# A four-layer encoder trunk: the two halves of a seven-product down-projection, product by product

## The reference

```python
for i in range(DEPTH):
    h = _rmsnorm(x, norm_mix[i])
    y = ...                      # mixer i % 3
    x = x + y
    x = x + _squared_relu_mlp(_rmsnorm(x, norm_mlp[i]), mlp_w1[i], mlp_w2[i])
return _rmsnorm(x, norm_final)

def _squared_relu_mlp(h, w1, w2):          # w1: 1024 x 4096, w2: 4096 x 1024
    return jnp.square(jax.nn.relu(h @ w1)) @ w2
```

## Time and profile before

| | |
|---|---|
| median of three runs | 2018.82 us (2018.57 to 2020.11) |
| the profiled execution's own time | 2018.45 us |
| its span, first to last instruction | 2016.7 us |
| PE busy | 1975.1 us (98%) |
| DVE busy | 1572.5 us (78%) |
| ACT busy | 1100.7 us (55%) |
| POOL busy | 346.7 us (17%) |
| read from HBM | 248.21 MB |

### The profile page before, as it was taken

One profiled execution on the slowest core, in us unless ns is written; L12 is line 12 of the kernel. 1 busy time (PEld: TensorE's weight loads), 2 busy tenths in 40 slices (PEclk: granted clock), 3 DMA queues, 4 the chain that ended last, 5 costly groups with the idle time before them and its releaser, 6 DMA issues.

```text
span 2016.7 us, 31611 instructions
## 1 busy us (share of the span) xinstructions
PE 1975.1 (98%) x12912; PEld 1779.3 (88%) x12912; DVE 1572.5 (78%) x1898; ACT 1100.7 (55%) x1540; POOL 346.7 (17%) x403
## 2 busy tenths in 40 slices
PE   9999999999999999999999999999999999999998
PEld 7888899999878889999888889999988888899997
DVE  7866878885898878887598786888687758688874
ACT  6655534545466645455456663554647646354463
POOL 7002001110200201113731201111731011011100
PEclk9999999999999999999999999999999999999999
DMA  6122457765222266667332145685632123468761
GB/s 192 63 67 72 140 136 167 194 141 162 89 85 91 87 157 157 159 155 184 119 88 71 58 151 139 165 205 141 169 86 71 57 69 126 110 166 189 173 189 42
DMA packets 232352, 256.31 MB, mean 127 GB/s; under 512 B 19632, under 2 KB 191216, under 8 KB 232208
## 3 DMA queue, kind: packets, MB, share of 16 engines
q1 hardware_dynamic: 183024, 207.01, 32.2%
q0 software_dynamic: 46784, 45.89, 14.6%
q10 hardware_dynamic: 2400, 1.38, 0.2%
HBM read 248.21 MB, written 2.10 MB: 124 GB/s over the span
## 4 chain that ended last, share of the span: by engine, by line
PE 84%; DVE 11%; ACT 3%; issue 2%; DMA 0%; SPq 0%; DVEq 0%; ACTq 0%
PE psum L772 26%; PE psum L774 25%; PE psum L773 25%; DVE w_lo L1611 2%; PE psum L1245 2%; DVE u_lo L1844 1%; ACT w_hi L2663 1%; DVE arena_r L1844 1%; DVE x L1901 1%; PE psum L1218 1%; DVE arena L1850 1%; PE psum L1353 1%; DVE h_lo L1638 1%; PE psum L1194 1%; PE psum L1190 1%
## 5 line engine op out<-in xcount | busy, mean ns | idle before, releaser
L1611 DVE TENSOR_TENSOR w_lo<-w_raw,w_hi 128x1024 fp32r<-128x1024 f32 x339 | 415.1, 1232 | 193.7 <-ACT w_hi L2663 192.3
L2663 ACT ACTIVATE w_hi<-w_raw 128x1024 fp32r<-128x1024 f32 x343 | 358.4, 1058 | 367.3 <-PE psum L774 237.4
L772 PE MATMUL psum<-u_hi,w_hi 128*128 128x512 f32 (+1 forms) x1256 | 439.9, 350 | 12.0 <-DVE u_lo L1844 7.4
L772 PE MATMUL psum<-h_hi,w_hi 128*128 128x256 f32 (+1 forms) x1368 | 440.6, 322 | 1.1 <-DVE w_lo L1611 1.1
L773 PE MATMUL psum<-h_lo,w_hi 128*128 128x256 f32 (+1 forms) x1368 | 437.3, 320 | 0.0
L774 PE MATMUL psum<-h_hi,w_lo 128*128 128x256 f32 (+1 forms) x1368 | 437.3, 320 | 0.0
L774 PE MATMUL psum<-u_hi,w_lo 128*128 128x512 f32 (+1 forms) x1256 | 433.9, 345 | 0.0
L773 PE MATMUL psum<-u_lo,w_hi 128*128 128x512 f32 (+1 forms) x1128 | 398.4, 353 | 0.0
L773 PE MATMUL psum<-arena_r,w_hi 128*128 128x256 f32 x1184 | 331.8, 280 | 0.0
L772 PEld LDWEIGHTS psum<-h_hi,w_hi 128*128 128x128 f32 x1368 | 260.1, 190 | 21.1 <-DVE w_lo L1611 1.6
L773 PEld LDWEIGHTS psum<-h_lo,w_hi 128*128 128x128 f32 x1368 | 260.4, 190 | 19.1 <-issue 1.2
(11 more groups left out here) (380 smaller groups left out, 3208.0 us busy)
## 6 DMA issues: line engine op xcount, KB each, us to landing
w_raw<-in_mlp_w SPq DMA_DIRECT2D x204, 512.0 KB, 4.9
arena<-in_mlp_w SPq DMA_DIRECT2D x92, 512.0 KB, 4.9
w_raw<-in_mlp_w POOLq DMA_DIRECT2D x52, 512.0 KB, 6.1
arena<-in_mlp_w POOLq DMA_DIRECT2D x28, 512.0 KB, 6.0
w_raw<-in_mla_w_o SPq DMA_DIRECT2D x16, 512.0 KB, 3.5
w_raw<-in_lru_w_in SPq DMA_DIRECT2D x16, 512.0 KB, 4.0
w_raw<-in_swa_w_in SPq DMA_DIRECT2D x12, 512.0 KB, 3.9
w_raw<-in_mla_w_ukv SPq DMA_DIRECT2D x8, 512.0 KB, 4.2
```

What stands on the lines that cost most here:

```text
L772: nc.tensor.matmul(out, stat[0], mov[0], start=start, stop=False, skip_group_check=skip)
L1611: ins = nc.vector.tensor_tensor(w_lo[:, to], tile, exact(w_hi[:, to]), ALU.subtract)
L2663: nc.scalar.activation(w_hi[:, to], raw_tile(op.raw), ACT.Copy).then_inc(w_hi_done, 1)
```

## The change

`seven_down(0)` and `seven_down(1)` become one `both_down`. PE now runs the first product of half 0, the first of half 1, the second of half 0, and so on; each left operand serves two products in a row. All four areas are claimed within the first four products. `weight_plan` lists operands and transfers in the new order. DVE's queue is written anew: a split for each product, the additions to `x` by halves, and the four areas freed after the last four products, in the order 1, 3, 0, 2. Its operand UT4 is made after U22 instead of before. Neither the number of matmuls nor that of the other instructions changes.

```diff
-    def seven_down(i, s, g):
+    def both_down(i, s):
...
-        a, e, b, p, q = blocks_of(block)
-        raws.extend((a, q, b, p, e))
...
+        halves = blocks(0), blocks(1)
+        for order in (0, 4, 2, 3, 1):
+            raws.extend(half[order] for half in halves)
+        for a, e, b, p, q in halves:
+            ops.append(Operand("A11", a))
+            a.freed = len(ops)
+        for a, e, b, p, q in halves:
+            ops.append(Operand("A21+A22", q))
+            q.freed = len(ops)
+        for a, e, b, p, q in halves:
+            ops.append(Operand("A12", b))
+        for a, e, b, p, q in halves:
+            ops.append(Operand("A11+A21", p, (p, e)))
+        for g, (a, e, b, p, q) in enumerate(halves):
+            ops.append(Operand("A11+A21+A22", p, made=sums + 1 + g))
+            down_sums.append((b, p))
+        for a, e, b, p, q in halves:
+            ops.append(Operand("A22", e))
+            p.freed = e.freed = len(ops)
+        for g, (a, e, b, p, q) in enumerate(halves):
+            ops.append(Operand("A11+A12+A21+A22", b, made=sums + 3 + g))
+            b.freed = len(ops)
+        sums += 4
...
+X_FIRST, X_V, X_Y, X_Z, X_SECOND = (1, 2), (3, 5), (7, 8), (9, 10), (11, 13)
...
+            def both_down():
...
+                halves = (0, 1), (2, 3)
+                for g, (xy, own) in enumerate(halves):
+                    claim(xy)
+                    pe.wait_ge(u_turned, n + 1)
+                    group(bank(xy, 0), U11, False)
+                for g, (xy, own) in enumerate(halves):
+                    claim(own)
+                    pe.wait_ge(u_turned, n + 2)
+                    group(bank(own, 1), UT1, False)
...
+                for g, (xy, own) in enumerate(halves):
+                    pe.wait_ge(u_turned, n + 7)
+                    pe.wait_ge(x_added, 7 * d + X_SECOND[g] + 1)
+                    group(bank(xy, 0), U22, True)
...
+            def both_down(n):
...
+                u_low(n, 3, U21)
+                dve.wait_ge(u_squared, 4 * n + 4)
+                nc.vector.tensor_tensor(kept[0][1], kept[0][1], kept[1][1], ALU.subtract).then_inc(u_turns, 1)
+                dve.wait_ge(u_high, 7 * n + 2)
+                nc.vector.tensor_tensor(minus_t1, minus_t1, kept[1][1], ALU.subtract).then_inc(u_turns, 1)
+                split(1)
                 product_passed()
...
+                add_first(0)
+                u_low(n, 4, UT3)
+                dve.wait_ge(u_turns, 4 * n + 3)
+                nc.vector.tensor_tensor(kept[1][0], kept[1][0], minus_t1, ALU.add).then_inc(u_turns, 1)
                 product_passed()
...
+                add_first(1)
+                split(1)
+                u_low(n, 5, UT2)
                 product_passed()
+                split(1)
+                add_v(0)
+                u_low(n, 6, U22)
                 product_passed()
...
+                split(1)
+                add_v(1)
+                u_low(n, 7, UT4)
+                product_passed()
+                split(1)
+                add_y(0)
+                product_passed()
+                split(1)
+                add_y(1)
+                product_passed()
                 add_blocks(*down_sums[d])
...
+                split(1)
+                add_z(0)
                 product_passed()
+                add_blocks(*down_sums[d + 1])
+                split(1)
+                add_z(1)
                 product_passed()
+                add_second(0)
+                split(1)
                 product_passed()
+                add_second(1)
+                split(1)
+                product_passed()
+                free(add(x21[0], Z[0], X_SECOND[0] + 1), 1)
+                split(1)
+                product_passed()
+                free(add(x21[1], Z[1], X_SECOND[1] + 1), 3)
+                split(1)
+                product_passed()
+                free(add(x12[0], X[0], X_V[0] + 1), 0)
+                split(1)
+                product_passed()
+                free(add(x12[1], X[1], X_V[1] + 1), 2)
+                split(1)
```

More of the change, by code:

```diff
@@ L201, in seven, with blocks @@
         sums += 2
-    def seven_down(i, s, g):
+    def both_down(i, s):
         nonlocal sums
-        def block(half, n):
-            return ("w2_block", i, s * SLICE + half * T, g * T + n, BLOCK)
-        a, e, b, p, q = blocks_of(block)
-        raws.extend((a, q, b, p, e))
[L212 to L224, removed]
+        def blocks(g):
+            return blocks_of(lambda half, n: ("w2_block", i, s * SLICE + half * T, g * T + n, BLOCK))
+        halves = blocks(0), blocks(1)
[21 more added lines that the diff above has]
+        sums += 4
     def first_seven(blocks):
@@ L952, in seven_products @@
                 group(bank(xy, 0), H22, True)
-            def seven_down(g):
-                xy, own = (0, 1) if g == 0 else (2, 3)
+            def both_down():
                 d = c.now("downs")
-                c.add("downs")
+                c.add("downs", 2)
                 n = 7 * (d // 2)
[L960 to L979, removed]
+                halves = (0, 1), (2, 3)
[8 more added lines that the diff above has]
+                for g, (xy, own) in enumerate(halves):
+                    pe.wait_ge(u_turned, n + 3)
+                    group(bank(xy, 1), U21, False)
+                for g, (xy, own) in enumerate(halves):
+                    pe.wait_ge(u_turned, n + 4)
+                    group(bank(own, 0), UT3, False)
+                for g, (xy, own) in enumerate(halves):
+                    pe.wait_ge(u_turned, n + 5)
+                    pe.wait_ge(x_added, 7 * d + X_FIRST[g])
+                    group(bank(xy, 0), UT2, True)
+                for g, (xy, own) in enumerate(halves):
+                    pe.wait_ge(u_turned, n + 7)
+                    pe.wait_ge(x_added, 7 * d + X_Z[g])
+                    group(bank(own, 0), UT4, True)
+                for g, (xy, own) in enumerate(halves):
+                    pe.wait_ge(u_turned, n + 7)
+                    pe.wait_ge(x_added, 7 * d + X_SECOND[g] + 1)
+                    group(bank(xy, 0), U22, True)
@@ L1888, in scaled_round @@
                 split(1)
-            def seven_down(g, n):
-                xy, own = (0, 1) if g == 0 else (2, 3)
+            def both_down(n):
                 d = c.now("downs")
[L1894 to L1897, removed]
+                c.add("downs", 2)
+                X, Y, Z, V = ([by_chunk(bank(a, b)) for a in areas] for areas, b in
+                              (((0, 2), 0), ((0, 2), 1), ((1, 3), 0), ((1, 3), 1)))
+                x11, x12, x21, x22 = ([x_block(g, i, j) for g in range(2)] for i in range(2) for j in range(2))
                 def add(to, sums, after, op=ALU.add):
@@ L1901, in add @@
                     return nc.vector.tensor_tensor(to, to, sums, op)
[L1903 to L1908, removed]
-                product_passed()
@@ L1910, in seven_down, with add_first, add_v @@
[L1910 to L1915, removed]
+                def add_first(g):
+                    add(x11[g], X[g], 0).then_inc(x_added, 1)
+                def add_v(g):
+                    add(x22[g], V[g], 0, ALU.subtract).then_inc(x_added, 1)
+                    add(x12[g], V[g], 0).then_inc(x_added, 1)
@@ new lines, in add_y, with add_z, add_second @@
+                def add_y(g):
+                    add(x11[g], Y[g], X_FIRST[g]).then_inc(x_added, 1)
+                def add_z(g):
+                    add(x22[g], Z[g], X_V[g]).then_inc(x_added, 1)
+                def add_second(g):
+                    add(x22[g], X[g], X_Z[g], ALU.subtract).then_inc(x_added, 1)
+                    add(x21[g], X[g], 0, ALU.subtract).then_inc(x_added, 1)
+                u_low(n, 3, U21)
+                dve.wait_ge(u_squared, 4 * n + 4)
+                nc.vector.tensor_tensor(kept[0][1], kept[0][1], kept[1][1], ALU.subtract).then_inc(u_turns, 1)
@@ L1942, in seven_down @@
                 split(1)
-                for a in (own, xy):
+                product_passed()
[7 more added lines that the diff above has]
+                split(1)
+                for a in range(4):
                     dve.wait_ge(area_free[a], c.now(f"area{a}"))
@@ L2001, in mlp @@
                             scaled_round(g, n)
-                        for g in range(2):
-                            seven_down(g, n)
+                        both_down(n)
                         continue
@@ L2895, in scaled_round, with both_down @@
                 square_in_place(other)
[L2897 to L2904, removed]
+            def both_down(n):
                 split(1)
[L2906 to L2909, removed]
+                act.wait_ge(u_turns, 4 * n + 2)
+                u_high_of(UT3)
+                act.wait_ge(u_turns, 4 * n + 3)
+                u_high_of(UT2)
                 split(1)
[L2911 to L2915, removed]
+                act.wait_ge(u_squared, 4 * n + 4)
+                u_high_of(U22)
+                split(1)
```

(7 more changed lines are left out.)

24 lines of the change are left out of this document (4 added, 20 removed).

## The result

The changed kernel takes 2063.77 us, median of four runs (2062.11 to 2065.53), beside 2018.76 for the kernel before: a ratio of 1.0221 with a 95% interval of 1.0208 to 1.0234. It is slower by 45.0 us, 5.6 us for each of the eight pairs.

A forecast was written before the change was run, and what follows sets the result against it. PE, busy 98% of the span, bounds the kernel; after the change DVE has no slack and the exit chain decides. 2018.8 + 28.4 (3.55 us for each of eight pairs) + 12 for the clock = 2059 us, range 2027 to 2092.

The forecast's parts named there:

- waits for `u`: PE's waits in half 0 for DVE's low parts of `u` (14.6 and 3.4 us) all go.
- waits inside the pair: PE waits for DVE's splits before the eighth and ninth product: 0.5 and 1.7 us, plus 0.7 from the entry.
- SP and plain load: After the eleventh operand's split: SP issues the load ahead (0.5 us), operand 70's load lands in 5.1 us.
- The entry: Pair's start: second of two adding transfers lands near 316.0, ACT's split and all DVE's queue 0.7 us late.
- The middle: Inside the pair: DVE's 40.4 us against PE's 40.3; waits cost 2.2 us instead of 4.7, 2.9 with the entry.
- The exit: Next round's first claim, area 0, waits behind operand 70's split: PE ready at 43.2, starts at 48.6, 5.4 us wait.
- The clock: PE's clock falls to half in most exit waits: 2.0 us at six of eight exits, 12 us.
- the one in which the clock holds: Rival: clock holds through exit waits of 5 us or falls too late to matter: 2047 us, chance 0.25.
- the light: Rival: exit transfers run nearly alone (6.0 us), no entry delay: 0.7 us a pair, 2024 us, chance 0.10.
- the fast case: Rival: exit load and adding transfer at fastest seen, 3.8 and 5.6 us: 1.0 us less a pair, 2011 us, chance 0.06.
- The crowded one: Rival: second adding transfer 2.6 us late at entry, 10.1 us at exit: 7.3 us a pair, 2093 us, chance 0.14.
- The fit of the Trainium skill: Adding transfer of 512 KB takes 2.0 us plus bytes over 436 GB/s, 3.2 us; kernel would end near 2002 us.

The follow-up runs named there:

- The filler: 20 matmuls of 512 columns into a free bank added behind each pair, against the changed kernel: 2050.49 us, ratio 1.0163 to the kernel before.
- the new order of DVE above: Changed kernel with DVE's order in the pair rewritten: splits and sums of blocks first, additions of V and Y last: 1998.58 us, ratio 0.9893 to the kernel before.

## Why the prediction was right

The forecast was 2059 us, the result 2063.8. By its steps, for the first pair, with t = 0 at 313.37:

| step | forecast | measured |
|---|---|---|
| waits for `u` | gone | gone |
| DVE's queue begins | 4.0 | 3.85 (317.22) |
| waits inside the pair | 1.2 + 1.7 | 0.89 + 1.49 |
| PE ends the pair | 43.2 | 43.2 |
| eleventh operand split | 30.5 | 30.3 (343.67) |
| SP and plain load | 5.6 | 6.4 |
| adding transfer | 8.2 | 8.3 |
| PE starts the round | 48.6 | 49.4 (362.78) |
| wait at the exit, mean of eight | 5.4 | 5.6 |

(The forecast of 1.2 us is its 0.5 and the 0.7 us of the entry.) The mean wait is 44.8 / 8. Over all eight pairs the round starts 47.65 to 49.41 us after the pair's first product, 48.5 on average, where the forecast had 48.6.

- *The entry.* The second adding transfer landed so that ACT began at 316.13, where I had put 316.0. That is the first pair. In five of the eight DVE's queue is no later than in the kernel before, and the mean of the eight is 0.2 us where I had charged 0.7. Without the transfer the kernel gains some 3 us, 0.4 us a pair.
- *The middle.* DVE's queue is as tight as its count of instructions said. These waits do not matter by themselves: the sum counts only the moment at which the next round starts, and the move of the additions of V bears that out.
- *The exit.* Removing the transfer, and moving the free ahead of it, each take away all of the loss. This was argued before and is shown now. The sum had 3.55 us a pair, 28.4 in all. By PE's start times the way from the pair's first product to the next round's first has grown by 27.6 us over the eight pairs, 3.46 each. Two small errors offset each other: the entry was charged too much, and the adding transfer took 7.9 to 9.1 us, 8.4 on average, where I had taken 8.2, with a plain load of 6 us ahead of it in two pairs.
- *The clock.* I charged 2.0 us at six of eight exits, 12 us. The filler shows 12 to 13 us. By PE's start times the eight first products of a round have grown by 15.9 us, 2.0 each. So the size was right, though it came from rows that only half fit, matmuls and transposes of float32: that is luck in part. The count was low: the eight waits are of 4.9 to 6.4 us, and the clock fell at all eight, for 6.8 us at seven of them and 3.4 at one. The forecast's 2.7 us of idleness before the fall was one case; here it is 2.0 to 4.6.
- *Together*, 27.6 and 15.9 us give 43.5 of the 43.6 us by which the spans of the two profiled executions differ. The medians differ by 45.0.

Of the rivals, the one in which the clock holds fell with the clock rows, and the light and the fast case with the adding transfer's 8.3 us. The crowded one was right about the entry's transfer, 11.4 us from issue to landing, but DVE's queue began only 0.6 us late by it. The fit of the Trainium skill ("DMA: Bandwidth & Descriptors", "Anatomy of one DMA"), 3.2 us for such a transfer, is nowhere near: the quickest of the 80 in the changed kernel took 5.5 us.

The prediction named DVE's position of the free as part of the chain, and yet took the chain as the price of the change. Its own steps held the cure: a free that needs nothing late behind a split that does.

## What to carry to other kernels

When an order is changed so that more buffers are held at once, look at the first claim after it: what frees that buffer, and what stands ahead of it in that engine's queue. In a strict queue, put an instruction that others wait for ahead of one that waits for a transfer, and use work that nobody waits for as filling while the transfer is under way, but no more of it than the wait is long: the new order of DVE above is left with 1 us of wait behind its filling. A gain inside a stretch counts only if it moves the instruction that starts the next chain.

## What was not expected of the hardware

Extra matmuls made the kernel faster: 20 for each exit, 160 in all, won 12 to 13 us, and the clock stayed at full (mean 1.000 in the profile, 0.997 to 0.999 in the other runs). When the clock had fallen, it was at half for 6.8 us in the first pair, of which PE worked for 5.3.

Adding transfers that overlap are slow. Of two of 512 KB issued 1.5 us apart at the entry the first took 5.8 us and the second 11.4; the median of all 80 in the kernel before is 6.0, in the changed one 7.6. Over the eight pairs the second took 8.8 to 11.4 us. The plain loads around them pay as well: the one issued 5.0 us before the first pair took 8.6 us, and 4.7 in the run without the second adding transfer. How much of a transfer's time is owed to which of its neighbours, no run separates.

```profile
w_raw<-in_mlp_w POOLq DMA_DIRECT2D x1, 512.0 KB, 5.8
arena<-in_mlp_w POOLq DMA_DIRECT2D x1, 512.0 KB, 11.4
```
